# Rows and conditioning chunks loaded within the last MLP block, and one semaphore clear over a range

## The reference

```
def layer(x, c, w_ada, b_ada, ...):
    mod = (jax.nn.silu(c) @ w_ada + b_ada)[:, None, :]
    sh1, sc1, g1, sh2, sc2, g2 = jnp.split(mod, 6, axis=-1)
    u = layer_norm(x) * (1 + sc1) + sh1
    ...
    x = layer_norm(ALPHA * x + g1 * (o @ w_out)) * ln1_g + ln1_b
    u = layer_norm(x) * (1 + sc2) + sh2
    f = jnp.square(jax.nn.relu(u @ w1)) @ w2
    x = layer_norm(ALPHA * x + g2 * f) * ln2_g + ln2_b
    return x, state
```

## Time and profile before

| | |
|---|---|
| time, median of 3 runs | 3314.0 us (3313.53 to 3315.84) |
| time of the profiled execution | 3317.91 us |
| its span, first to last instruction | 3316.1 us |
| PE busy | 2945.9 us (89%) |
| DVE busy | 1611.6 us (49%) |
| POOL busy | 1525.3 us (46%) |
| ACT busy | 882.9 us (27%) |

### The profile page before, as it was taken

How to read it: one execution, slowest core, us unless ns; L and a number is a source line. 1 busy time by engine, 2 the same in 40 slices (tenths; PEclk the granted TensorE clock), 3 DMA queues, 4 the chain that set the end, 5 groups by cost and what they waited for, 6 DMA issues and landing times. The chain is left out here.

```text
span 3316.1 us, 47501 instructions
## 1 busy us (share of the span) xinstructions
PE 2945.9 (89%) x18646; PEld 2809.0 (85%) x18646; DVE 1611.6 (49%) x3403; ACT 882.9 (27%) x1768; POOL 1525.3 (46%) x692
## 2 busy tenths in 40 slices
PE   6888899869799999999688888997779999999992
PEld 6887889656799999999688787895659999999992
DVE  6352498556533333333473416884665333333346
ACT  1332366424300110001153315663252110011001
POOL 2675388124344343443237835961243434434334
PEclk6998999889899999999669999998889999999995
DMA  6342111223111111110533412113311111111103
GB/s 244 127 148 75 62 45 49 88 81 128 53 51 38 51 49 39 51 38 25 214 122 126 156 39 76 43 42 108 132 60 57 51 38 51 39 50 51 38 13 117
DMA packets 117547, 254.18 MB, mean 77 GB/s; under 512 B 42628, under 2 KB 79016, under 8 KB 103892
## 3 DMA queue, kind: packets, MB, share of 16 engines
q1 hardware_dynamic: 111348, 230.15, 20.1%
q10 hardware_dynamic: 6048, 22.02, 2.0%
HBM read 217.45 MB, written 42.45 MB: 78 GB/s over the span
## 5 line engine op out<-in xcount | busy, mean ns | idle before, releaser
L375 PE MATMUL psum<-u_hi,w_hi 128*128 128x352 f32 x2016 | 655.8, 325 | 39.3 <-POOLq L358 39.3
L375 PE MATMUL psum<-u_lo,w_hi 128*128 128x352 f32 x2016 | 655.5, 325 | 0.0
L375 PE MATMUL psum<-u_hi,w_lo 128*128 128x352 f32 x2016 | 654.8, 325 | 0.0
L2071 DVE SCALAR_TENSOR_TENSOR acc_t<-psum,mods,acc_t 128x704 f32<-128x704 f32 x720 | 376.1, 577 | 274.4 <-PE psum L375 274.4
L375 PE MATMUL psum<-h_hi,w_lo 128*128 128x352 f32 x1536 | 495.3, 322 | 0.0
L375 PE MATMUL psum<-h_lo,w_hi 128*128 128x352 f32 x1536 | 495.0, 322 | 0.0
L375 PE MATMUL psum<-h_hi,w_hi 128*128 128x352 f32 x1536 | 494.3, 322 | 0.0
L354 POOL CAST w_hi<-w_raw 128x2048 fp32r<-128x2048 f32 (+1 forms) x88 | 170.1, 1933 | 653.5 <-DVEq L2064 356.7
L356 POOL TENSOR_TENSOR w_lo<-w_raw,w_hi 128x2048 fp32r<-128x2048 f32 (+1 forms) x88 | 434.3, 4935 | 7.1
L2054 DVE TENSOR_TENSOR h_relu<-h_relu 128x1056 f32<-128x1056 f32 x64 | 113.1, 1767 | 634.2 <-ACT h_relu L2044 634.2
L375 PEld LDWEIGHTS psum<-u_hi,w_hi 128*128 128x128 f32 x2016 | 383.0, 190 | 41.4 <-POOLq L358 41.1
(11 more groups left out here) (257 smaller groups left out, 5623.1 us busy)
## 6 DMA issues: line engine op xcount, KB each, us to landing
w_raw<-in_w_all SPq DMA_DIRECT2D x86, 1024.0 KB, 4.8
w_ada_b<-in_w_ada_t ACTq DMA_DIRECT2D x42, 512.0 KB, 3.6
w_ada<-in_w_ada_k SPq DMA_DIRECT2D x13, 1024.0 KB, 18.1
w_ada_v<-in_w_ada_t SPq DMA_DIRECT2D x22, 512.0 KB, 3.3
row_tiles<-in_x_prompt SPq DMA_DIRECT2D x16, 512.0 KB, 7.4
scr_o<-o_head SPq DMA_DIRECT2D x32, 256.0 KB, 2.6
row_tiles<-scr_o SPq DMA_DIRECT2D x16, 512.0 KB, 7.1
x_between_norms<-row_tiles SPq DMA_DIRECT2D x16, 512.0 KB, 2.6
```

Source lines behind the costliest of these rows:

```text
L375: mm = pe.matmul(out[:, b, :], w[s][:, c:c + P], a[:, k, b * NB:(b + 1) * NB], start=(k == 0 and w is w_hi and a is a_hi), stop=(k == n - ...
L2071: ins = dve.scalar_tensor_tensor(a, y, mods[:, 40 + m, c:c + 1], a, ALU.mult, ALU.add)
```

## The change

Three parts. (1) Within the MLP block SP, after the last weight chunk, waits for the stores of the rows between the norms and for `h_mm` to reach 152 (the end of down 14), and then loads the nine row tiles into a tensor of their own, `mlp_rows`, which lies where the MLP's input was; after layer 0 it also loads the first three conditioning chunks. DVE's `sum_rows` reads its rows from there. (2) The eight conditioning chunks of layer 1 share three buffers. Chunk n >= 3 is issued after a wait for PE to be done with chunk n-3, and the five such issues stand between the stores of the first tiles, in SP's one queue. (3) The 114 clears become one over the range of their numbers.

```diff
--- before.py
+++ after.py
@@ -138,6 +138,8 @@
         Q0 = U0 + 67584
 
         ada_w = [at(f"w_ada{s}", U0 + s * 8192, [P, CW]) for s in range(max(ADA_PE))]
+        mlp_x = at("mlp_rows", U0, [P, NTT, D])
+        ada_r = [at(f"w_ada_r{s}", U0 + 36864 + 8192 * s, [P, CW]) for s in range(3)]
         ada_a = [at(f"w_ada_a{s}", U0 + ADA_PE[0] * 8192 + s * 4096, [P, D]) for s in range(ADA_SLOTS)]
         c_rows = at("c_rows", Q0 + 8448, [P, 2, D])
         ada_junk = at("ada_products", Q0 + 16640, [P, D])
@@ -255,7 +257,7 @@
         pro_ext, pro_edges, pro_x = sem("pro_ext_loaded"), sem("pro_ext_edges"), sem("pro_selectors_loaded")
         row_x = [sem(f"x_rows_loaded{t}") for t in range(NTT)]
         ada_mm = sem("ada_chunks_done")
-        ada_ch = [sem(f"ada_chunk_loaded{s}") for s in range(ADA_PE[0] + 1)]
+        ada_ch = [sem(f"ada_chunk_loaded{s}") for s in range(ADA_PE[0])]
         ada_in = [sem(f"ada_loaded{s}") for s in range(ADA_SLOTS)]
         ada_used, pro_c, pro_c_out = sem("ada_used"), sem("pro_condition"), sem("pro_condition_stored")
 
@@ -575,17 +577,27 @@
                 act.activation(x, x, ACT.Identity, bias=rsb[0:r, 3, t:t + 1], scale=rsb[0:r, 4, t:t + 1]).then_inc(done, 1)
 
         def sp_chunks(sp, l, first=0, last=None):
-            for s in range(ADA_PE[l])[first:last]:
-                sp.dma_start(ada_w[s][:], io["w_ada_k"][l, s]).then_inc(ada_ch[min(s, ADA_PE[0])], 16)
+            for n in range(ADA_PE[l])[first:last]:
+                if l == 0:
+                    sp.dma_start(ada_w[n][:], io["w_ada_k"][l, n]).then_inc(ada_ch[n], 16)
+                else:
+                    if n >= 3:
+                        sp.wait_ge(ada_mm, sum(ADA_PE[:l]) + n - 2)
+                    sp.dma_start(ada_r[n % 3][:], io["w_ada_k"][l, n]).then_inc(ada_ch[n % 3], 16)
 
         def pe_chunks(pe, l, first, last):
 
             for n in range(first, last):
-                pe.wait_ge(ada_ch[min(n, ADA_PE[0])], 16 * (l + 1) if n < ADA_PE[0] else 16 * (ADA_PE[l] - ADA_PE[0]))
+                if l == 0:
+                    w = ada_w[n]
+                    pe.wait_ge(ada_ch[n], 16)
+                else:
+                    w = ada_r[n % 3]
+                    pe.wait_ge(ada_ch[n % 3], 16 * (2 + n // 3))
                 for m in (2 * n, 2 * n + 1):
                     for k in range(KT):
                         c0 = 256 * k + P * (m % 2)
-                        mm = pe.matmul(psum[:, 6, 2 * m:2 * m + 2], ada_w[n][:, c0:c0 + P], c_silu[:, k, :],
+                        mm = pe.matmul(psum[:, 6, 2 * m:2 * m + 2], w[:, c0:c0 + P], c_silu[:, k, :],
                                        start=(k == 0), stop=(k == KT - 1))
                 mm.then_inc(ada_mm, 1)
 
@@ -712,7 +724,7 @@
                     act.wait_ge(f_st[(k - 3) % 4], stored(k - 3, u))
                     norm(k - 3, f_xn)
 
-        def chain_dve(own, u, loaded, gate, after_sums, final):
+        def chain_dve(own, u, rows, loaded, gate, after_sums, final):
 
             dve = own.eng
 
@@ -727,7 +739,7 @@
                 if gate is not None:
                     own.did(dve.tensor_tensor(out, out, gate(t), ALU.mult))
                     own.settle()
-                own.did(dve.scalar_tensor_tensor(x, x, ALPHA, out, ALU.mult, ALU.add), f_ev)
+                own.did(dve.scalar_tensor_tensor(x, rows[0:r, t, :], ALPHA, out, ALU.mult, ALU.add), f_ev)
                 own.settle()
                 first_figures(t)
 
@@ -807,10 +819,10 @@
                 mm.then_inc(f_mm, 1)
                 between(t)
 
-        def mlp_rows_loaded(sp, l, first, last):
+        def mlp_rows_loaded(sp, first, last):
 
             for t in range(first, last):
-                sp.dma_start(x_all[0:rows_of(t), t, :], scr_x1[t * P:t * P + rows_of(t), :]).then_inc(row_x[t], 16)
+                sp.dma_start(mlp_x[0:rows_of(t), t, :], scr_x1[t * P:t * P + rows_of(t), :]).then_inc(row_x[t], 16)
 
         def second_norm(sp, l):
 
@@ -907,13 +919,12 @@
                 with nc.Block() as block:
                     @block.sync
                     def _(sp):
-                        mlp_rows_loaded(sp, l, 0, 2)
                         second_norm(sp, l - 1)
-                        mlp_rows_loaded(sp, l, 2, NTT)
-                        sp_chunks(sp, l, 0, 2)
                         begin_sp(sp, l)
-                        sp_chunks(sp, l, 2)
-                        chain_stores(sp, 0, lambda t: x_rows(l, t), 0, NTT)
+                        for t in range(NTT):
+                            if t + 3 < ADA_PE[l]:
+                                sp_chunks(sp, l, t + 3, t + 4)
+                            chain_stores(sp, 0, lambda t: x_rows(l, t), t, t + 1)
 
                     @block.gpsimd
                     def _(pool):
@@ -939,7 +950,7 @@
                     @block.vector
                     def _(dve):
                         own = Own(dve, dve_step)
-                        chain_dve(own, 0, 16 * (3 * l + 1), None, lambda: None, False)
+                        chain_dve(own, 0, mlp_x, 16 * (3 * l + 1), None, lambda: None, False)
                         own.settle()
                         dve.wait_ge(ada_mm, sum(ADA_PE[:l + 1]))
                         add_bias(own, l, 0, 16, psum[:, 6, 0:32].rearrange("p (m c) -> p m c", c=2), 8)
@@ -1960,7 +1971,7 @@
                     own.settle()
                     split_turned_rows(own, 1, g_out, None)
 
-                    chain_dve(own, USE, 16 * (3 * l + 3), lambda t: gate_p[:] if t < NPT else gate_s[:],
+                    chain_dve(own, USE, x_all, 16 * (3 * l + 3), lambda t: gate_p[:] if t < NPT else gate_s[:],
                               lambda: dve.sem_inc(w_used, OUT_CH), False)
 
 
@@ -1984,6 +1995,11 @@
                 def _(sp):
                     sp_weights(sp, l, UP0 + 1, 1)
                     sp_weights(sp, l, UP0 + 2, 2 * MLP_BLK - 2)
+                    chain_stored(sp, USE + 1)
+                    sp.wait_ge(h_mm, 10 * MLP_BLK - 8)
+                    mlp_rows_loaded(sp, 0, NTT)
+                    if l + 1 < DEPTH:
+                        sp_chunks(sp, l + 1, 0, 3)
 
                 @block.gpsimd
                 def _(pool):
@@ -2077,16 +2093,15 @@
 
             nc.all_engine_barrier()
             counts.clear()
-            for s in all_sems:
-                nc.gpsimd.sem_clear(s)
+            numbers = sorted(s.num for s in all_sems)
+            assert numbers == list(range(numbers[0], numbers[-1] + 1))
+            nc.gpsimd.sem_clear(range(numbers[0], numbers[-1] + 1))
             nc.all_engine_barrier()
 
         with nc.Block() as block:
             @block.sync
             def _(sp):
-                mlp_rows_loaded(sp, DEPTH, 0, 2)
                 second_norm(sp, DEPTH - 1)
-                mlp_rows_loaded(sp, DEPTH, 2, NTT)
                 chain_stores(sp, 0, lambda t: x_rows(DEPTH, t), 0, NTT)
                 chain_stored(sp, 1)
 
@@ -2107,7 +2122,7 @@
 
             @block.vector
             def _(dve):
-                chain_dve(Own(dve, dve_step), 0, 16 * (3 * DEPTH + 1), None, lambda: None, True)
+                chain_dve(Own(dve, dve_step), 0, mlp_x, 16 * (3 * DEPTH + 1), None, lambda: None, True)
 
 
 _OUT_SHAPES = {
```

## The result

The changed kernel takes 3282.5 us (median of 4 runs, 3281.3 to 3284.3) where the kernel before takes 3314.1 us (4 runs, 3313.5 to 3315.8): ratio 0.9904, 95% interval 0.9887 to 0.9921, or 31.6 us less. The profiled execution took 3283.8 us with a span of 3281.8 us, against 3317.9 and 3316.1.

The account below looks back on a forecast made before the run. The prediction saw time lost at layer ends to serial clears and to loads starting only when their readers do. Savings of 16.6 + 3.7 + 11.6 = 31.9 us off 3314.0 gave 3282 us, range 3277 to 3292.

Parts of the forecast that it names:

- The clears: At two barriers, one range clear replacing 114 single clears was to save 16.6 us in all.
- the two bounds: For one clear over 114 semaphores: 0.04 us, or 114 times 0.07 us; the lower was taken.
- The loads cost nothing in the MLP block: In the MLP's last block, 7.5 MB of loads taking 22 us were to be covered by PE, costing nothing.
- The final stage: First sum 2.05 us after the final stage's start instead of 5.75, saving 3.7 us to the end.
- my clock rival: Full PE clock at the start of both stages: tile 0 about 0.9 us sooner at each, 3280 us; chance 0.10.
- The middle stage: Step-by-step schedule of DVE's sums: the last moves from 77.4 to 65.8 us after the stage's start, saving 11.6 us.
- The bias: The norm's bias load arrives late for POOL at both places, 1 to 3.4 us each, 3284 to 3289 us; chance 0.13.
- The new waits: In the middle stage, stores queued behind chunk issues that wait for PE were to cost nothing.
- the ring: Three shared chunk buffers bound the middle stage, slower than before: 3326 us if loads take 45 us; chance 0.02.

Follow-up runs that it names:

- the run with the late issue: Changed kernel with rows and chunks issued some 6 us before the end of the last MLP block's work instead of 23 us; one execution 3290.4 us.
- the loads alone: Changed kernel with the 114 single semaphore clears put back, so only the load moves remain; 3302.7 us, ratio 0.9962.
- the run with the chunks alone early: Changed kernel with row tiles loaded at the start of the middle and final stages, only three chunks loaded in the last MLP block; 3290.3 us, ratio 0.9921.
- the rows alone: Changed kernel with the first three chunks issued at the middle stage's start behind gain and bias; medians 3286.4 us, then 3283.6 us when repeated.

## Why the prediction held

The forecast of 3282 us was met to 0.5 us, with 3 us between the runs, and that closeness is luck in part: the clears fell short by 1.2 us, the final stage gained 0.9 more than forecast, and the blocks outside the sum moved by 2.8 us in all. What held is the mechanism, term by term.

**The clears** (16.6 us; measured 15.4). The step that was mis-sized is the range clear itself: I took the lower bound of 0.04 us because a clear of one number bore the range instruction's name, and it is 0.655 us. The name said nothing of how the price grows with the range; the two bounds, 0.04 and 8 us, were right to be kept.

**The loads cost nothing in the MLP block.** Shown: the stretch with DMA share 0.85 has PE's and DVE's busy time and counts of before, and layer 1's MLP block, with the rows in it, took 756.6 us where it took 756.7. The mean rate there, 324 GB/s, is close to the 339 of the earlier trace rows that the term was worked out with; the run with the late issue shows what lies beyond the cover.

**The final stage** (3.7; measured 4.6, and 3.7 with the loads alone). The step, a first sum 2.05 us after the start in place of 5.75, was right for the clock it assumed: 2.1 with the loads alone, where the transposes ran at the lower level. In the changed kernel they ran at the upper one and the sum began at 1.2; that was the 0.9 us of my clock rival, at one of its two places. How much of the 5.75 is due to the load's place is open by up to 1.9 us (the run with the chunks alone early).

**The middle stage** (11.6; measured 11.5). The whole schedule of sums held to 0.2 us. Two of its claims, that POOL's splits set the pace behind tile 3 and that PE is ahead of it, are shown by moving the splits (9.8 us) and by delaying the chunks (nothing lost, and 2 us lost once the splits were gone). What the sum did not say is that its gain has no single owner: it is 11.5 with the rows alone and 9.7 with the chunks alone.

**The bias** (the first rival, 0.13) did not come: in the changed kernel it took 5.8 us, and POOL's first tile was released by ACT. Loads issued 6 us before the block's last matmul ended show it in full.

**The new waits** cost nothing: in the middle stage no engine waited for a DMA, where before ACT had waited 8.0 us for a store. With one buffer the ring binds; two buffers were not run.

## What to carry to other kernels

A load whose reader starts a stage belongs under the last work of the stage before, if the data and a place for it are there; issue it early enough that the small loads that follow it in the same queue are not late, for these are then what costs. Where two kinds of loads share a queue, ask which of them is waited for: here, in the middle stage, moving either one brought most of what moving both did. And sum a stage's steps one by one with the engine that sets each: the schedule that gave 65.8 us also named what to take next, POOL's splits, worth 9.8 us of that stage.

## What had not been expected of the hardware

A semaphore clear over a range takes longer the more numbers it has: 44 ns for one, 352 for 57, 655 for 114.

The clock after a short pause. PE stands still for 3.3 us at either place before the transposes (the prediction had 2.7, with a clear of 0.04 us). In the changed kernel the clock was at 1.2 GHz for most of the middle stage's transposes, which took 4.35 us (granted clock 0.61 over 1604.16 to 1608.40), and at 2.4 GHz for the final stage's (1.00 over 3219.9 to 3223.6). The Trainium skill ("TensorE: Matmul & The Clock Gate", Part 1: The HAM clock gate) has half rate as what the array falls back to when idle. After the 11 us of idleness in the kernel before, and in the one with the loads alone, the first transposes of both stages ran at half rate (granted clock 0.50 or 0.51), as the Trainium skill has it; after the short pause both happened. Of nine profiled executions with early rows and a range clear (pauses of 3.3 to 3.7 us), eight began the final stage at the upper level (first sum 1.2 us after the start) and one, with the rows alone early, at the lower (2.1), while in the middle stage the first sum began at 1.6 to 2.1 us in all nine. Why the two places differ stays open. In the middle stage, moreover, PE was busy for all of 57 us at 1.2 GHz:

```profile
1613.00:1670.00 57.00, 57.00 (x272) 56.56 (x273) 53.94 (x84) 33.25 (x66) 44.61 (x18) 0.50 0.46 159
```
